# A hybrid decoder layer on eight cores: conv chain off GpSimd, five more buffers for x, eight token tiles turned by DMA

## What is computed

```python
def trunk_layer(x, c, pool_buf, conv_buf, ffn_buf, pos0, ...):
    mod = (silu(c) @ w_ada + b_ada)[:, None, :]
    sh1, sc1, gt1, sh2, sc2, gt2 = jnp.split(mod, 6, axis=-1)
    h = rmsnorm(x, g_pre_mix) * (1 + sc1) + sh1
    v_pool, x_conv, gate_b, gate_c = split(h @ w_in)            # 512 columns each
    y_pool = pool_mixer(concat(pool_buf, v_pool), pos0, pool_w, pool_scale)
    conv_in = concat(conv_buf, gate_c * x_conv)
    y_conv = gate_b * causal_dwconv(conv_in, conv_w)            # three taps
    x = x + gt1 * rmsnorm(concat(y_pool, y_conv) @ w_out, g_post_mix)
    h2 = rmsnorm(x, g_pre_ffn) * (1 + sc2) + sh2
    a, b = split(causal_dwconv(concat(ffn_buf, h2 @ ffn_w_up), ffn_conv_w))
    return x + gt2 * rmsnorm((silu(a) * b) @ ffn_w_down, g_post_ffn), states
```

## Time and profile before

| | us |
|---|---|
| median of 3 runs | 727.05 (726.73 to 730.04) |
| the profiled execution | 730.44 |
| its span, slowest core (core 7) | 728.9 |
| spans of the other cores | 722.9 to 727.2 |
| PE busy on core 7 | 701.2 (96%) |
| DVE busy | 464.1 (64%) |
| ACT busy | 327.0 (45%) |
| POOL busy | 273.1 (37%) |
| PE busy with products with zeros | 21.8 (82 matmuls) |

### The profile page before, as it was taken

The page is one execution under the profiler, slowest core; times in us unless marked ns, Lnnn a source line. Parts: engine busy times, 40 slices in busy tenths (PEclk is TensorE's granted clock), DMA queues, the critical chain, the costliest instruction groups (busy, mean ns, idle before and its releaser), DMA issues.

```text
span 728.9 us, 12128 instructions; the slowest of 8 cores (722.9 to 728.9 us)
## 1 busy us (share of the span) xinstructions
PE 701.2 (96%) x4072; PEld 332.2 (46%) x4072; DVE 464.1 (64%) x614; ACT 327.0 (45%) x585; POOL 273.1 (37%) x288
## 2 busy tenths in 40 slices
PE   6899898999999989999999999999999999999996
PEld 3445443444454434444444444445444444444443
DVE  2769588545589978777777511127777777758403
ACT  3355654454677664444445211134545444433111
POOL 1101377333777634333544232222442424223320
PEclk9999999899999999999999999999999999999999
DMA  8999788997989466465889964113424433052332
GB/s 226 184 226 182 185 149 132 196 180 153 206 277 282 158 116 116 85 136 94 146 150 158 213 230 145 58 58 58 76 42 95 80 58 59 1 198 96 134 112 73
DMA packets 23533, 100.72 MB, mean 138 GB/s; under 512 B 3184, under 2 KB 3696, under 8 KB 18608
## 3 DMA queue, kind: packets, MB, share of 16 engines
q0 software_dynamic: 9072, 47.71, 38.8%
q1 hardware_dynamic: 14400, 52.23, 22.5%
HBM read 127.02 MB, written 20.63 MB: 203 GB/s over the span
## 4 chain that ended last, share of the span: by engine, by line
PE 73%; DMA 12%; DVE 4%; issue 4%; POOL 3%; ACT 2%; DVEq 0%; SPq 0%; POOLq 0%; ACTq 0%
PE ps L526 71%; DMA big<-x 4%; DMA y<-big 2%; DMA scp<-w_scp 2%; DMA ring<-w_inc 2%; POOL big L565 1%; PE ps L536 1%; DMA bigp<-x 1%; DMA big<-xs 1%; DMA wsh<-w_sh 1%; ACT big L557 1%; DVE s L946 1%; DVE big L561 1%; DVE ta L561 1%; DVE xnp L570 0%
## 5 line engine op out<-in xcount | busy, mean ns | idle before, releaser
L526 PE MATMUL ps<-ah,ring 128*128 128x512 bf16 (+2 forms) x2240 | 409.1, 343 | 3.5 <-DVE q L561 1.2
L526 PEld LDWEIGHTS ps<-ah,ring 128*128 128x128 bf16 x2240 | 188.4, 98 | 215.0 <-issue 9.8
L561 DVE SCALAR_TENSOR_TENSOR big<-ps,misc,big 128x1023 f32<-128x1023 f32 (+1 forms) x176 | 224.4, 1281 | 74.3 <-ACT halob L557 34.9
L565 POOL TENSOR_TENSOR g<-big 128x1024 bf16<-128x1024 f32 x44 | 103.9, 2363 | 167.1 <-DVE big L565 82.4
L557 ACT ACTIVATE big<-ps,misc 128x1024 f32<-128x1024 f32 x88 | 98.0, 1114 | 144.2 <-PE ps L526 142.4
L526 PE MATMUL ps<-wdn,g 128*128 128x512 bf16 x704 | 153.1, 379 | 0.0
L565 POOL TENSOR_TENSOR big<-big 128x256 f32<-128x256 f32 (+2 forms) x51 | 65.6, 1287 | 124.0 <-DVE big L561 102.0
L526 PEld LDWEIGHTS ps<-wdn,g 128*128 128x128 bf16 x704 | 68.5, 98 | 82.1 <-issue 0.4
L557 ACT ACTIVATE big<-ps 128x1024 bf16<-128x1024 f32 (+2 forms) x30 | 29.0, 965 | 124.0 <-PE ps L526 115.9
L674 DVE RECIPROCAL stat<-stat 128x1 f32<-128x1 f32 (+1 forms) x64 | 9.7, 158 | 102.2 <-ACT stat L557 101.8
L526 PE MATMUL ps<-wo,by 128*128 128x512 bf16 x256 | 57.4, 379 | 0.0
(11 more groups left out here) (143 smaller groups left out, 520.4 us busy)
## 6 DMA issues: line engine op xcount, KB each, us to landing
ring<-w_up POOLq DMA_DIRECT2D x22, 1024.0 KB, 9.5
y<-big SPq DMA_DIRECT2D x27, 512.0 KB, 3.1
big<-y SPq DMA_DIRECT2D x16, 512.0 KB, 4.2
big<-x SPq DMA_DIRECT2D x7, 1024.0 KB, 9.3
big<-x SPq DMA_DIRECT2D x12, 512.0 KB, 7.9
wdn<-w_down POOLq DMA_DIRECT2D x11, 512.0 KB, 11.8
wg<-w_gate POOLq DMA_DIRECT2D x4, 1024.0 KB, 10.5
scp<-w_scp POOLq DMA_DIRECT2D x8, 384.0 KB, 7.1
```

What stands on the lines that cost most here:

```text
L526: inst = e.matmul(bank_ap, l, r, start=(first and i == 0), stop=(last and i == len(pairs) - 1))
L561: return K.op(eng, lambda e: e.scalar_tensor_tensor(out, in0, s, in1, op0, op1), reads=reads, writes=writes, cost=c_dve(n))
L565: return K.op(eng, lambda e: e.tensor_tensor(out, in0, in1, op), reads=reads, writes=writes, cost=c_dve(n) if eng == "dve" else c_pool(n))
```

## The change

- `conv_mid`: the POOL add is gone. `TA` = w2*q stays on ACT, w1*q and w0*q are added by two DVE instructions, and the last product reads B from PSUM with its bias (DVE), so `TB` and its ACT copy are gone and B's bank is held until then. The small copies of carried columns go from POOL to ACT.
- `pool_win`: group 0 (window 2) is one subtraction instead of an add and a combination; the factor 1/2 goes into the pool map. The window sums of the samples go from POOL to DVE.
- `norm_tile`: tiles 8 to 16 of the mixing stage are scaled on ACT instead of DVE. `ada_vec` writes its two results with ACT instead of DVE.
- Five more buffers `EX` for x, over regions of the mixing stage that are free by then; `XB` names the buffer of each tile. Eleven of the 17 x loads of the output projection now wait for no store: tiles 0 to 10 have eleven different buffers, and tiles 11 to 16 take those of tiles 0 to 4 and 8.
- Tiles 8 to 15 are no longer turned on PE in the output projection. `turn_by_dma` turns each by one DMA transpose from SBUF to SBUF, two after each of the first four steps of the first down projection, and `modulate` for them is there too. The loads of `USB` and of the first up weights of group 1 move from step 2 to steps 4 and 5.
- The last tile's down projection is cut into pieces of 512, 384 and 128 columns instead of two of 512.
- `PROJ` is another order, and `Sched.order` now lets a DVE or POOL operation with `port` wait for the other in full, or takes another first.

```diff
-m:0,0 P:3,1 T:16 O:2,1 T:12 M:2 S W:0,1 m:0,1 m:0,4 m:1,4 m:1,0 P:0,2 I O:1,1 C W:1,0 W:2,1 T:13 W:3,0 T:14
+m:0,0 W:0,0 T:12 W:2,0 S O:3,0 W:1,0 m:0,4 O:1,1 P:3,1 O:0,1 W:3,0 v:0,0 P:2,2 P:0,2 W:2,1 m:1,0 I T:13 T:14
...
+    EX = [alloc("ex", [128, D], F32, at=g_at + 4096 * i) for i in range(5)]
...
+        if k == ST1 and t > 7:
+            act(N[0:rows, :], X[0:rows, :], AF.Copy, [r_x, r_stat[k + 1][t]], [r_n], D, scale=STAT[0:rows, k + 1, t:t + 1])
...
             if g == 0:
-                tt(S, V[:, 16:528], V[:, 15:527], ALU.add, [rV], [r_s[g]], n)
+                tt(Y, V[:, 15:527], V[:, 16:528], ALU.subtract, [rV], [r_by[g][c]], n)
...
-            act(TB[k], B, AF.Identity, [rb, r_cb[j]], [r_tb[k]], n, bias=hb)
-            free(rb)
...
         act(sh(TA[k]), v[2], AF.Copy, [rq, r_vecs], [r_ta[k]], n, scale=w2)
-        act(sh(XC[k]), v[0], AF.Copy, [rq, r_vecs], [r_xc[k]], n, scale=w0)
-        tt(TA[k][:, 0:n], TA[k][:, 0:n], XC[k][:, 0:n], ALU.add, [r_ta[k], r_xc[k]], [r_ta[k]], n, eng="pool")
-        stt(sh(TA[k]), v[1], w1, sh(TA[k]), ALU.mult, ALU.add, [rq, r_ta[k], r_vecs], [r_ta[k]], n)
+        for m, w in ((1, w1), (0, w0)):
+            stt(sh(TA[k]), v[m], w, sh(TA[k]), ALU.mult, ALU.add, [rq, r_ta[k], r_vecs], [r_ta[k]], n)
         if c < 4:
-            tt(BY[:, 4 + j, c0:c0 + n], TA[k], TB[k], ALU.mult, [r_ta[k], r_tb[k]], [r_by[4 + j][c]], n)
+            stt(BY[:, 4 + j, c0:c0 + n], B, hb, TA[k], ALU.add, ALU.mult, [r_ta[k], rb, r_cb[j]], [r_by[4 + j][c]], n)
+            free(rb)
...
+    XB = [0, 1, 2, 3, 7, 13, 10, 9, 6, 11, 12, 0, 1, 2, 3, 7, 6]
...
-            if t < FIRST_T:
+            if t < 8:
                 turn_tile(t, o_xn[t], "act" if t % 2 else "dve")
...
+    LAST = [(0, 512), (512, 896), (896, 1024)]
...
-        if step == 2:
+        if step < 4:
+            for t in (8 + 2 * step, 9 + 2 * step):
+                turn_by_dma(t, d_op[-1])
+        if step == 4:
+            r_usb.alias(r_xnp)
+            up_load(1, 0)
+        if step == 5:
             ffn_state_in()
-            up_load(1, 0)
             up_load(1, 1)
```

155 lines of the change are left out of this document (89 added, 66 removed).

## The result

The changed kernel takes **717.23 us** (median of 4 runs, 716.71 to 719.38), the kernel before 728.38 us beside it (726.73 to 730.04). The ratio is 0.9852, with a 95% interval of 0.9817 to 0.9888. The forecast was 715.5 us, in a range of 709.5 to 724.0. Run again as a reference for the last experiments, it gave 717.98 us beside 731.29 and a ratio of 0.9823 (0.9798 to 0.9849).

> The changed kernel itself, run beside the next three on one chip, as their reference: ratio to the kernel before 0.985, within its interval of 0.982 to 0.989.

A forecast was written before the change was run, and what follows sets the result against it. PE's work and clock were taken as the bound at 130 to 178 and from 262 us, with idle PE between. Terms 4 + 3.6 + 3.5 + 1.7 + 0.3 = 13.1 us, taken as 11.5 from 727.05, gave 715.5 us, range 709.5 to 724.0.

The forecast's parts named there:

- Turns, waits and clock: Output projection: without PE turns of tiles 8 to 15, 3.6 us of work, 3.5 of waits and 1.7 of clock go.
- The DMA transposes: First down projection: eight transposes of 256 KB, 4.2 us each, cost nothing; rival over 7.8 us is slower, chance 0.07.
- In series: First down projection: DMA transposes taken one after another, T us each, with T taken as 4.2.
- the limit of 7.8 us a tile: First down projection: the longest DMA transpose time, in series, at which group 1 still starts on time.
- The mixing stage (4 us): 74 to 178 us: 4 us gained, between 3.1 and 6.3, bounds 0 and 9.9; no-gain rival, chance 0.20.
- the hole of 2.5 us: Queue of casting loads before the first `w_ss` load: gap made by POOL's arithmetic, claimed to go, about 2.5 us.
- the 6.3 us of that case: Mixing stage, rival that PE alone sets it: fold starts 6.3 us earlier, 711 us in all, chance 0.12.
- The conv chain: 74 to 130 us: PE waits for DVE's q, 3.2 us at longest; without POOL's adds the chain can feed PE.
- its 8.4 us: Conv chain: estimated excess of DVE operations lying beside POOL operations, 8.4 us, at least 5.0, claimed to go.
- become the bound: Conv chain, rival: DVE makes PE wait as much as before, total within 0.5%, 723.4 to 730.7 us, chance 0.11.
- The gate rows: Before the first tail: later gate matmuls leave 22 us for 1.8 on DVE plus store and load, about 13 + 7.
- The last piece (0.3 us): End of kernel: ACT's last square over 128 columns instead of 512 gains 0.3 us, bounds 0 and 0.5.

The follow-up runs named there:

- the last experiments: Three runs beside the kernel before: changed kernel with old order string and gate matmuls late, 1.003; with gate load cut in two, 0.982; with last tile in two, 0.982.
- with the gates early: Changed kernel with only the gate matmuls moved 112 products of 512 columns (24 us) earlier: 723.0 us, ratio 0.994 to the kernel before.

## Why the prediction was right, and where it was not

The time and its direction were right, for the turns and what hangs on them by the stated mechanism, and for the mixing stage by luck of the size.

**Turns, waits and clock (3.6 + 3.5 + 1.7 = 8.8 us)** held. The stages show 8.3, undoing the transposes cost 0.9970 − 0.9852 in ratio, 8.6 us, and adding them alone to the kernel before gave 728.4 − 720.2 = 8.2. That the clock would stay up without the waits is shown too: from 252 to 268 us it is 0.89 to 0.91 on seven of eight cores with the turns, and 1.00 on all without them. What was left unsaid is that this is nearly the whole gain. Between the kernel before with the transposes and the whole change lie 0.989 and 0.985 (0.982 in the second run), 2.4 to 4.5 us. And the sum treats the terms as if they added up, which the experiments deny: undoing the transposes, the POOL add or the buffers costs 8.6, 6 to 8 and 11 us, together far more than the gain.

**The DMA transposes** cost nothing, as forecast, with 3.2 us to landing at the median where 4.2 was taken. "In series" was wrong: they overlap, so there was far more room than the limit of 7.8 us a tile said. The first two passed that limit, 10.3 and 9.5 us, and PE had no gap; in series at such a time group 1 would have started late.

**The mixing stage (4 us)** came to 3.8, but the step that led there failed. It said that `w_out` would land 3 us later than before, because one more `w_ss` load stands ahead of it, and that it "cannot be hurried". It landed 3.9 us earlier on the slowest cores, 2.2 at the median. The sum counted POOL's queue and left SP's out: the loads of x that ran beside `w_out` now wait for the gate matmuls' buffers. The gate matmuls were priced only for the chain behind them, and not for the buffers ahead. Nor did the hole of 2.5 us close: the first `w_ss` load landed at 115.4 + 11.2 = 126.6 us, against 127.1 before. What made up for the sixth load is that all six were in at 118.0 + 28.3 = 146.3, where five had been in at 146.5. The landing was worth less than the forecast thought, besides: with the gates early `w_out` landed at 166.8 on the slowest core, near the forecast's 166.0, and the output projection began only 0.7 us later at the median of the cores. In the changed kernel the gate was open and PE alone set the stage, and of the 6.3 us of that case 3.8 came. Some 1.1 us were lost before the second conv weights: with 376 products to go the changed kernel was at 160.6 on the scale where the one before was at 159.5 (start plus the remaining products at 0.2155 us). In 9 to 74 us PE is idle longer and the clock lower than before (0.92 and 0.97 on the two slowest cores), where the forecast left this stretch as it was. The rest of the difference is not accounted for.

**The conv chain** was read rightly as far as it names POOL's adds; they cost 6.3 us in the new order. But the forecast priced the drawn-out passes, and the larger part is the wait for the sum: 7.5 us of idle DVE in the earlier trace rows, which its 8.4 us leave out, and 19.2 us with the add back. DVE did not become the bound at 46 of 56 us, though from 74 to 178 us it is busy 5.2 us more and not 1.7, in part with work that now falls into this time. The claim that the gain depends on the load behind it is what the run with the new chain alone shows, with 3.93 us of waiting for `w_out`.

**The gate rows** "just fit" in the forecast and came 3.3 us too late. Their store took 7.2 us and the slowest load 11.6, together 19 where 20 was expected. But SP issued the store 3.6 us after the gate matmuls ended (156.2), where 1.8 was taken, and the last load only at 168.6, 1.6 us behind the store's landing: the whole chain took 24.0 us. And the room was 20.8 us and not 22, since the first tail's norm was ready at 177.0, 7.3 us into the output projection, where the forecast took 10. It costs 1.3 to 1.5 us of waiting, and removing it gained nothing.

**The five buffers** had no term of their own. Taken out of the changed kernel they take its whole gain along, while the kernel before with the transposes has most of the gain without them. This is the largest thing the forecast did not see, and its cause stays open.

**The last piece (0.3 us)** gave 0 to 0.1: the shorter square was right, the read of the sum ahead of it was missed. Not forecast either is the 0.5 us of group 1.
